# Activations of a PEER expert layer: high and low part of the tokens in one 512-column matmul, halves added on VectorE

## What is computed

```
def chunk(args):
    hc, ec, gc = args
    u = expert_u[ec]
    act = jax.nn.gelu(jnp.einsum('td,thkd->thk', hc, u), approximate=False)
    return jnp.einsum('thk,thkd->td', gc * act, expert_v[ec])
```

## Time and profile before

| | us |
|---|---|
| median of 3 runs | 3625.66 (3624.41 to 3626.98) |
| the profiled execution, its own time | 3627.83 |
| its span in the trace | 3626.0 |
| matmuls of `activations`, 6144 | 779.9 busy |
| matmuls of `combine`, 3072 | 745.3 busy |
| `v_low` / `u_low`, 256 each, VectorE | 313.7 / 311.8 busy |
| `v_high` / `u_high`, 256 each, ScalarE | 268.3 / 267.3 busy |

### The profile page before, as it was taken

How to read it: one execution, slowest core, us unless ns; L and a number is a source line. 1 busy time by engine, 2 the same in 40 slices (tenths; PEclk the granted TensorE clock), 3 DMA queues, 4 the chain that set the end, 5 groups by cost and what they waited for, 6 DMA issues and landing times.

```text
span 3626.0 us, 50298 instructions
## 1 busy us (share of the span) xinstructions
PE 3126.6 (86%) x17474; PEld 2603.7 (72%) x17474; DVE 1969.6 (54%) x3674; ACT 1103.8 (30%) x1439; POOL 185.7 (5%) x294
## 2 busy tenths in 40 slices
PE   6877279999999897845899999995899798899798
PEld 2546269999999735534799999994876496776496
DVE  1236986666666503399766666664553364553363
ACT  0011134444444301002444444441432142432142
POOL 0000260000000000005300000000000000000000
PEclk9978699999999998878999999997999899899899
DMA  7421005555555572110355555554333354323254
GB/s 266 170 93 70 0 27 188 186 188 187 185 185 186 194 298 105 70 47 0 96 188 186 188 187 185 185 186 142 127 116 114 113 176 178 123 104 132 107 184 139
DMA packets 123917, 525.86 MB, mean 145 GB/s; under 512 B 18552, under 2 KB 26616, under 8 KB 95648
## 3 DMA queue, kind: packets, MB, share of 16 engines
q1 hardware_dynamic: 109600, 502.58, 40.7%
q10 hardware_dynamic: 14208, 21.83, 1.8%
HBM read 523.29 MB, written 1.06 MB: 145 GB/s over the span
## 4 chain that ended last, share of the span: by engine, by line
issue 85%; DVE 10%; PE 2%; DVEq 1%; POOL 1%; ACTq 0%; DMA 0%; ACT 0%; POOLq 0%
DVE slab L1799 3%; PE prob_ps L893 1%; DVE arena L1729 1%; DVE arena L1720 1%; DVE arena L1723 1%; PE acc L674 1%; DVE slab L1802 1%; DVE arena L1726 1%; DVE arena L1717 1%; POOL small L1473 1%; DVE arena L1766 0%; DVE arena L1760 0%; ACTq L1135 0%; DVE arena L1769 0%; PE turn_ps L724 0%
## 5 line engine op out<-in xcount | busy, mean ns | idle before, releaser
L908 PEld LDWEIGHTS prob_ps<-hTr,utr 128*128 128x128 f32 x6144 | 773.5, 192 | 26.1 <-ACT utr L1260 6.4
L908 PE MATMUL prob_ps<-hTr,utr 128*128 128x256 f32 x6144 | 779.9, 283 | 6.1 <-DVE utr L1811 6.1
L919 PE MATMUL acc<-vr,wtr 128*128 128x512 f32 x3072 | 745.3, 391 | 5.3 <-DVE vr L1829 5.3
L919 PEld LDWEIGHTS acc<-vr,wtr 128*128 128x128 f32 x3072 | 560.5, 188 | 112.3 <-issue 6.4
L1829 DVE TENSOR_TENSOR vr<-slab,vr 128x1024 fp32r<-128x1024 f32 x256 | 313.7, 1225 | 512.7 <-ACT vr L1274 512.7
L1274 ACT CAST vr<-slab 128x1024 fp32r<-128x1024 f32 x256 | 268.3, 1048 | 607.1 <-PE acc L919 607.1
L1811 DVE TENSOR_TENSOR utr<-slab,utr 128x1024 fp32r<-128x1024 f32 x256 | 311.8, 1218 | 5.8 <-ACT utr L1260 5.8
L724 PE MATMUL turn_ps<-ident,arena 128*128 128x128 f32 (+1 forms) x336 | 69.5, 371 | 267.3 <-DVE arena L1769 130.5
L1260 ACT CAST utr<-slab 128x1024 fp32r<-128x1024 f32 x256 | 267.3, 1045 | 0.0
L724 PEld LDWEIGHTS turn_ps<-ident,arena 128*128 128x128 f32 (+1 forms) x336 | 52.4, 187 | 287.0 <-DVE arena L1769 130.9
L791 PE MATMUL acc<-slab,arena 128*128 128x512 f32 x384 | 176.7, 618 | 55.6 <-DVE arena L1641 37.4
(11 more groups left out here) (200 smaller groups left out, 4380.6 us busy)
## 6 DMA issues: line engine op xcount, KB each, us to landing
slab<-in_pack_b SPq DMA_DIRECT2D x132, 1024.0 KB, 4.9
slab<-in_peer_u SPq DMA_DIRECT2D x256, 512.0 KB, 4.3
slab<-in_peer_v SPq DMA_DIRECT2D x256, 512.0 KB, 3.3
slab<-in_pack_a SPq DMA_DIRECT2D x84, 1024.0 KB, 6.7
arena<-in_b_ada ACTq DMA_DIRECT2D x2, 3072.0 KB, 12.7
slab<-in_pack_b SPq DMA_DIRECT2D x4, 832.0 KB, 5.3
arena<-in_norm_g ACTq DMA_DIRECT2D x4, 512.0 KB, 14.1
arena<-in_k_pool ACTq DMA_DIRECT2D x2, 1024.0 KB, 13.1
```

The source lines that it names most:

```text
L908: ins = pe.matmul(prob_ps[:, m % 2, 0:S], utr[:, m % 2, uh, k * P:k * P + P], hTr[:, hh, k, :], start=(k == 0 and n == 0), stop=(k == KD - ...
L919: ins = pe.matmul(y_ps[:, t, n, :], wtr[:, m % 2, wh, t * P:t * P + P], vr[:, vh, n * 512:n * 512 + 512], start=first and k == 0, stop=las ...
```

## The change

Activations. For each block of D the two products with U's high part become one matmul: its moving operand is `hTr[:, :, k, :]`, the tokens' high part and their low part side by side, 512 columns, and its result fills a whole bank. The product of U's low part with the tokens' high part goes on top of the bank's first 256 columns. So 16 matmuls (8 of 512 and 8 of 256 columns) and 16 weight loads stand where 24 of 256 columns stood; the number of columns, 6144, stays. The activations are now the sum of the bank's two halves.

VectorE gets a new step, `halves`: it copies the second half of the bank to `ga`, drains, adds the first half, and raises `halves_added`. Gelu then reads `ga` and not the bank, in place. TensorE waits for `halves_added` where it waited for `gelu_done`; gelu's wait for `wt_ready` is gone. VectorE's order in the loop becomes u_low(i + 1), halves(i), v_low(i), weighted(i).

```diff
@@ -902,11 +903,12 @@
                     pe.wait_ge(*ut_act.at("a", l, i + 1))
                     pe.wait_ge(*ut_dve.at("a", l, i + 1))
                     if not (isinstance(i, int) and i < 2):
-                        pe.wait_ge(*gelu_done.at("a", l, i - 1))
+                        pe.wait_ge(*halves_added.at("a", l, i - 1))
                     for k in range(KD):
-                        for n, (uh, hh) in enumerate(HALVES):
-                            ins = pe.matmul(prob_ps[:, m % 2, 0:S], utr[:, m % 2, uh, k * P:k * P + P], hTr[:, hh, k, :],
-                                            start=(k == 0 and n == 0), stop=(k == KD - 1 and n == 2))
+                        pe.matmul(prob_ps[:, m % 2, :], utr[:, m % 2, 0, k * P:k * P + P], hTr[:, :, k, :],
+                                  start=(k == 0), stop=False)
+                        ins = pe.matmul(prob_ps[:, m % 2, 0:S], utr[:, m % 2, 1, k * P:k * P + P], hTr[:, 0, k, :],
+                                        start=False, stop=(k == KD - 1))
                     ins.then_inc(am_full.sem, 1)
 
                 def combine(i, m, first=False, last=False):
@@ -1260,11 +1262,8 @@
                     act.copy(utr[:, m % 2, 0], expert_u[:, m % 2]).then_inc(ut_act.sem, 1)
 
                 def gelu(i, m):
-                    act.wait_ge(*am_full.at("a", l, i + 1))
-                    if not (isinstance(i, int) and i < 2):
-
-                        act.wait_ge(*wt_ready.at("a", l, i - 1))
-                    act.activation(ga[:, m % 2, :], prob_ps[:, m % 2, 0:S], ACT.Gelu).then_inc(gelu_done.sem, 1)
+                    act.wait_ge(*halves_added.at("a", l, i + 1))
+                    act.activation(ga[:, m % 2, :], ga[:, m % 2, :], ACT.Gelu).then_inc(gelu_done.sem, 1)
 
                 def v_high(i, m, place):
@@ -1811,6 +1810,14 @@
                     dve.tensor_tensor(utr[:, m % 2, 1], expert_u[:, m % 2], utr[:, m % 2, 0].bitcast(F32),
                                       ALU.subtract).then_inc(ut_dve.sem, 1)
 
+                def halves(i, m):
+
+                    dve.wait_ge(*am_full.at("a", l, i + 1))
+                    dve.tensor_copy(ga[:, m % 2, :], prob_ps[:, m % 2, S:2 * S])
+                    dve.drain()
+                    dve.tensor_tensor(ga[:, m % 2, :], ga[:, m % 2, :], prob_ps[:, m % 2, 0:S], ALU.add)\
+                        .then_inc(halves_added.sem, 1)
+
                 def weighted(i, m):
 
                     dve.wait_ge(*gelu_done.at("a", l, i + 1))
@@ -1832,14 +1839,17 @@
                 u_low(0, 0)
                 for i in range(3):
                     u_low(i + 1, i + 1)
+                    halves(i, i)
+                    v_low(i, i)
                     weighted(i, i)
-                    v_low(i, i)
                 with dve.Fori(0, NKEYS // 4 - 1) as it:
                     for j in range(4):
                         i = it * 4 + (3 + j)
                         u_low(i + 1, j)
+                        halves(i, (3 + j) % 4)
+                        v_low(i, (3 + j) % 4)
                         weighted(i, (3 + j) % 4)
-                        v_low(i, (3 + j) % 4)
+                halves(NKEYS - 1, 3)
                 weighted(NKEYS - 1, 3)
                 v_low(NKEYS - 1, 3)
                 dve.wait_ge(*y_full.at("a", l, 1))
```

More of the change, by code:

```diff
@@ L257, in two_blocks @@
         gelu_done = Signal(sem("gelu_done"), a=NKEYS)
+        halves_added = Signal(sem("halves_added"), a=NKEYS)
         wt_ready = Signal(sem("wt_ready"), a=NKEYS)
```

## The result

The changed kernel takes 3895.96 us (median of 4, 3890.67 to 3903.27) against 3625.65: ratio 1.0753 (95% interval 1.0739 to 1.0768), 270 us slower. The forecast was 3897.

A forecast was written before the change was run, and what follows sets the result against it. TensorE's work (5.62 us per tile) was taken as the bound, just hiding the 5.39 us vr chain; with weighted the chain becomes 6.68. 135.6 us per layer, 271 for two, gave 3897 us, range 3862 to 3945 (chance 0.85).

The forecast's parts named there:

- The bound and the chain: Expert loops: combine's end, v_high, v_low, weighted, next combine set the step, 6.68 us per tile in place of 5.62.
- a last one: End of a layer: the old order stands there, so the last step is 5.39 + 0.09 us.
- The overlap of 0.09 us and the stalled combine: Chain per tile: minus 0.09 us as VectorE begins weighted early, plus 0.09 as a waited-for combine takes 3.00 us.
- Halves hidden: Each tile: halves on VectorE, about 0.9 us, costs nothing beside combine, with some 0.6 us left.
- TensorE's saving: Activations: eight fewer matmuls save 0.09 us per tile, hidden because the chain over vr is longer.
- The start of a layer: First tile of each layer: halves and weighted come ahead of combine(0), which starts 1.9 us later.
- The clock: Rival, expert loops: TensorE's waits lower the granted clock, 7.1 us per tile, about 4000 us; chance 0.06.
- Halves exposed: Rival, each tile: halves takes over 1.5 us, delaying gelu and v_high; about 4000 us; chance 0.04.
- Faster or unchanged: Rivals: VectorE's order doesn't matter, 3603 us, chance 0.03; or weighted adds 0.14 us, no change, chance 0.02.
- The sum: Whole kernel: 126 steps x 1.06, plus 0.1 and 1.9, is 135.6 us per layer, 271 for two.

The follow-up runs named there:

- wide_old_order: The changed kernel with weighted back ahead of v_low on VectorE; matmuls and halves as changed: 3623.64 us, ratio 1.0002 to the kernel before.
- narrow_old_order_b: Changed kernel with weighted back ahead of v_low and each 512-column activation matmul split into two of 256, halves kept: 3627.96 us, ratio 1.0018 to the kernel before.
- weighted_longer: The changed kernel with the cast of weighted and its drain done twice: 3993.55 us, ratio 1.102 to the kernel before.
- both longer halves: The changed kernel with the copy of halves and its drain done twice, and in another run four times: 3897.04 and 4074.23 us.
- halves_longer: The changed kernel with the copy of halves and its drain done twice: 3897.04 us, ratio 1.0761 to the kernel before.
- before_new_order: The kernel before with v_low ahead of weighted on VectorE, 24 matmuls and no halves: 3887.73 us, ratio 1.0729 to the kernel before.

## Why the prediction was right

**The bound and the chain.** Right. The step was forecast at 6.68 and is the 6.68 us mean over layer 0: combine(0) at 533.88 and the last one at 1382.21, 848.33 us for 127 steps. Each part was measured apart: v_low short by 0.53 gave 135 us (252 x 0.53 = 134), weighted longer by 0.37 gave 98 (252 x 0.37 = 93), weighted put back gave all 270. The mean holds a first step of 8.2 us (below) and a last one of 5.52 (5.48 forecast), which happen to even out; the 125 between them are 6.68 each.

**The overlap of 0.09 us and the stalled combine.** Both as taken from the earlier trace rows: weighted starts 0.09 before v_low's end, TensorE's first matmul comes 0.07 behind weighted's end, and the combine that was waited for takes 3.02 us.

**Halves hidden.** Right, and the slack is 0.75 where I had some 0.6.

**TensorE's saving.** Wrong in size, and harmless here: 0.09 us per tile was forecast, 0.03 came. I took the 229 ns of a combine's matmul for the merged one. The rows of `wide_old_order` have 0.22 and 0.12 us for one pair's starts (806.24, 806.46, 806.58), but the mean over eight pairs is 2.81 / 8 = 0.351, against 3 x 0.120 = 0.360. And combine, untouched, takes 2.78 in place of 2.75. In `narrow_old_order_b`, with halves but without the merging, it takes 2.75, so the 0.03 come with the merged matmuls; by what way was not tried. The activations alone are 2.81 in place of 2.87, 0.06 less. By the Trainium skill (TensorE: Matmul & The Clock Gate, Back-to-back issue gap) 20 ns per tile were estimated for them: the measured 60 lie between that and my 90, and its absolute gap for 256 columns (109 ns) is not the trace's 120.

**The start of a layer.** The term was 1.9 us, and by the rows it is that: first matmul of the activations to combine(0), 9.45 us (524.43 to 533.88) against 7.63, 1.8 more. The first tiles:

```profile
524.43 0.47 PE L908 MATMUL prob_ps<-hTr,utr 128*128 128x512 f32 x1 [3.06 <-DVE utr L1810]
...
529.05 0.42 DVE L1816 COPY arena<-prob_ps 128x256 f32<-128x256 f32 x1 [3.63 <-PE prob_ps L910]
...
529.55 0.42 DVE L1818 TENSOR_TENSOR arena<-arena,prob_ps 128x256 f32<-128x256 f32 x1
...
530.01 0.42 ACT L1266 ACTIVATE arena<-arena 128x256 f32<-128x256 f32 x1 [4.74 <-DVE arena L1818]
...
530.33 1.03 ACT L1273 CAST vr<-slab 128x1024 fp32r<-128x1024 f32 x1
...
533.39 0.43 DVE L1830 TENSOR_TENSOR wtr<-arena,wtr 128x256 fp32r<-128x256 f32 x1
...
533.88 4.53 PE L921 MATMUL acc<-vr,wtr 128*128 128x512 f32 x12 [2.09 <-DVE wtr L1830]
...
538.20 0.51 PE L908 MATMUL prob_ps<-hTr,utr 128*128 128x512 f32 x1
```

But the row of combine(0) shows 4.53 us for 12 matmuls, and the step behind it is 8.2 (533.88 to 542.06), not 6.7. The windows of this stretch:

```profile
530.00:537.00 7.00, 4.91 (x21) 3.76 (x20) 4.17 (x7) 2.72 (x4) 0.00 (x0) 0.86 0.31 95
537.00:545.00 8.00, 7.21 (x33) 5.81 (x32) 4.17 (x7) 2.42 (x3) 0.00 (x0) 0.91 0.40 139
```

In 530 to 537 us, where TensorE had waited 2.09 us for combine(0), the clock was granted at 0.86, and at 0.91 in 537 to 545: part of both was at the 1.2 GHz level, and 1.5 us were lost that I had not reckoned with. From 545 to 1370 us it is 1.00. Layer 1 goes the same way. The other traces do not settle the cause. In layer 0 combine(0) took 4.5 to 5.5 us in the four kernels in which TensorE had waited 2.09 to 3.96 us for it (the changed one, `weighted_longer`, both longer halves), and 3.0 in the seven in which it had waited 1.61 or less. But the length of the wait alone does not decide it: behind nearly the same wait the last combine of layer 0 took 3.00 us (granted 1.00 in 1382 to 1386 us) and that of layer 1 4.46 (0.76 in 2748 to 2755), and in the other kernels it took 3.0 or 4.2 to 4.6 as well.

```profile
1382.21 3.00 PE L921 MATMUL acc<-vr,wtr 128*128 128x512 f32 x12 [2.48 <-DVE vr L1836]
...
2750.57 4.46 PE L921 MATMUL acc<-vr,wtr 128*128 128x512 f32 x12 [2.49 <-DVE vr L1836]
```

**The rivals.** The clock did not fall in the loops, in spite of a wait in each tile: granted 1.00. The Trainium skill's warning (A second HAM failure mode: psum-queue depth-cycling, the same page) is thus not borne out by this loop. Around the expert loops a lower clock is seen at a layer's start and end, beside longer waits; whether a wait caused it was not tried. Halves exposed: excluded by `halves_longer`. Faster or unchanged: excluded by the result, and `before_new_order` shows that the order costs.

**The sum.** 271 us were forecast and 270 measured. The expert part, from the first matmul of the activations to the last combine, grew by 1.8 + 134.7 = 136.5 us in layer 0 and by 135.8 in layer 1 (1893.56 to 2750.57, before 1764.01 to 2485.24); 135.6 were forecast for each. The 134.7 hold the 1.5 us of the clock, which stood in no term of the sum. Together that is 272.3, and the span of the profiled execution grew by 265.8: the rest of the kernel, which the change doesn't touch, was 6.5 us shorter. That rest scatters between the profiled executions of all these kernels (511 to 517 us from the last combine of layer 0 to the first activations of layer 1, 1139 to 1146 behind the start of the last combine), so the closeness of the total to 1 us is partly luck.

## What to carry to other kernels

An in-order engine makes everything behind a wait as late as the wait. Before a step is moved, ask what the step ahead waits for: here two calls changed places, and weighted's 1.2 us of work that had been free, because it ran while TensorE multiplied, came to stand between the end of one matmul group and the start of the next. Where two cycles are nearly as long as each other (5.62 and 5.39 here), the shorter one is the one to look at, and the places where nothing else covers it, such as the end of the loop, show its length. And the saving from fewer matmuls at an equal number of columns was small here, 0.03 us of a step of 5.62: measure it with the chain out of its way before giving up anything for it.

## What the runs showed of the hardware

- Merging two 256-column matmuls with the same weights into one of 512 in two pieces saved 0.06 us of 2.87 per eight blocks, and the following 12 matmuls of 512 columns, the same as before, took 0.03 us more (2.78 in `wide_old_order`, 2.75 in `narrow_old_order_b`). Both were stable over a layer (steps of 5.593 and 5.619 us).
- A wait of 0.84 us in every tile of 6.7 us did not lower the granted clock (1.00 over 825 us); at a layer's start a wait of 2.09 us was followed by a lower one (0.86 in the 7 us around it), while behind one of 2.48 us at the end of layer 0 combine took 3.00 us, at 1.00.
